# Asking by name for one function table set at the head of six stages

## The reference

```python
log_1m = jnp.where(causal, jax.nn.log_sigmoid(-z), 0.0)          # stick-breaking, gates: log(1 + exp(-|z|))
y = xf * lax.rsqrt(jnp.mean(xf * xf, axis=-1, keepdims=True) + EPS)   # in the kernel exp(-0.5 * log(...))
dt = jax.nn.softplus(dt_raw.astype(jnp.float32) + dt_bias.astype(jnp.float32))
```

## Time and profile before

| | us |
|---|---|
| median of 3 runs | 3015.35 |
| lowest, highest | 3010.44, 3020.8 |
| profiled execution, its own time | 3026.64 |
| its span | 3024.8 |
| TensorE matmuls busy | 2710.7 |
| ScalarE busy | 684.2 |
| VectorE busy | 1305.2 |
| GpSimd busy | 1503.0 |

### The profile page before, as it was taken

One profiled execution on the slowest core, in us unless ns is written; L12 is line 12 of the kernel. 1 busy time (PEld: TensorE's weight loads), 2 busy tenths in 40 slices (PEclk: granted clock), 3 DMA queues, 4 the chain that ended last, 5 costly groups with the idle time before them and its releaser, 6 DMA issues. The chain is left out here.

```text
span 3024.8 us, 33325 instructions
## 1 busy us (share of the span) xinstructions
PE 2710.7 (90%) x11856; PEld 2109.7 (70%) x11856; DVE 1305.2 (43%) x1909; ACT 684.2 (23%) x1008; POOL 1503.0 (50%) x1022
## 2 busy tenths in 40 slices
PE   6897779999988998789988998989997989899996
PEld 4784447888857775468965874858875668678774
DVE  4953333222229999727202415242165213454442
ACT  2003652001133333411022104131022230200002
POOL 2543005666638887256622753416651256466651
PEclk7997789999999998899999998979999999999998
DMA  7531002323212222122320221112320022223221
GB/s 253 181 112 63 1 0 70 98 97 98 98 56 70 83 84 72 43 83 70 98 70 14 98 82 44 58 41 70 98 84 28 22 90 75 64 97 94 87 78 37
DMA packets 230474, 231.17 MB, mean 76 GB/s; under 512 B 9995, under 2 KB 228844, under 8 KB 230252
## 3 DMA queue, kind: packets, MB, share of 16 engines
q1 hardware_dynamic: 225968, 228.74, 23.6%
q10 hardware_dynamic: 4412, 1.24, 0.2%
HBM read 227.86 MB, written 2.10 MB: 76 GB/s over the span
## 5 line engine op out<-in xcount | busy, mean ns | idle before, releaser
L829 POOL TENSOR_SCALAR Wh<-raw 128x2048 fp32r<-128x2048 f32 (+3 forms) x197 | 367.5, 1866 | 1370.7 <-PE PS L873 1129.5
L835 POOL TENSOR_TENSOR Wl<-raw,Wh 128x512 fp32r<-128x512 f32 (+3 forms) x772 | 1026.7, 1361 | 29.2 <-issue 1.6
L873 PE MATMUL PS<-Hh,Wh 128*128 128x512 f32 (+2 forms) x2104 | 842.7, 401 | 117.7 <-DVE Hl L596 54.7
L873 PE MATMUL PS<-Hl,Wh 128*128 128x512 f32 (+2 forms) x2104 | 836.4, 398 | 0.0
L873 PE MATMUL PS<-Hh,Wl 128*128 128x512 f32 (+2 forms) x2104 | 835.3, 397 | 0.0
L873 PEld LDWEIGHTS PS<-Hh,Wh 128*128 128x128 f32 (+2 forms) x2104 | 402.5, 191 | 227.6 <-issue 90.1
L873 PEld LDWEIGHTS PS<-Hh,Wl 128*128 128x128 f32 (+2 forms) x2104 | 401.9, 191 | 90.6 <-issue 1.5
L873 PEld LDWEIGHTS PS<-Hl,Wh 128*128 128x128 f32 (+2 forms) x2104 | 403.1, 192 | 86.7
L873 PE MATMUL PS<-Bh,Wh 128*128 128x512 f32 x688 | 270.2, 393 | 17.8 <-DVE Bl L1851 9.1
L873 PE MATMUL PS<-Bl,Wh 128*128 128x512 f32 x688 | 269.0, 391 | 0.0
L873 PE MATMUL PS<-Bh,Wl 128*128 128x512 f32 x688 | 268.9, 391 | 0.0
(11 more groups left out here) (308 smaller groups left out, 2888.4 us busy)
## 6 DMA issues: line engine op xcount, KB each, us to landing
raw<-in_w_in SPq DMA_DIRECT2D x44, 1024.0 KB, 5.6
raw<-in_w_ff SPq DMA_DIRECT2D x32, 1024.0 KB, 5.3
raw<-in_conv_w_in SPq DMA_DIRECT2D x24, 1024.0 KB, 5.2
raw<-in_ret_w_in SPq DMA_DIRECT2D x24, 1024.0 KB, 5.2
spare<-in_ada_w SPq DMA_DIRECT2D x20, 1024.0 KB, 6.9
raw<-in_w_up SPq DMA_DIRECT2D x20, 1024.0 KB, 5.2
raw<-in_w_out SPq DMA_DIRECT2D x8, 1024.0 KB, 5.1
raw<-in_conv_w_out SPq DMA_DIRECT2D x8, 1024.0 KB, 5.3
```

The source lines that it names most:

```text
L829: pool.tensor_scalar(st.Wh[0:rows, slot, k, 0:g.width], st.raw_slot(slot)[0:rows, k, 0:g.width], 1.0, 1.0, ALU.mult, ALU.mult)
L835: ins = pool.tensor_tensor(st.Wl[0:rows, slot, k, 0:g.width], st.raw_slot(slot)[0:rows, k, 0:g.width], st.Wh[0:rows, slot, k, 0:g.width].b ...
L873: mm = pe.matmul(out, lhs, rhs, start=(k == 0 and n == 0), stop=(k == parts[-1][0] and n == 2))
```

## The change

At the head of ScalarE's program of six stages stands a request for one table set by name. Nothing else is touched.

```diff
+EXP_AND_LOG = "natural_log_exp_and_others"
...
+        act.preload_act_table_set(EXP_AND_LOG)     # attention_part
         for h in range(SH):
             softplus(h)
...
     def _(act):
+        act.preload_act_table_set(EXP_AND_LOG)     # retention_part
         for h in range(RET_HEADS):
             act.wait_ge(pv_done, h + 1)
...
+        act.preload_act_table_set(EXP_AND_LOG)     # gates_parts
         act.wait_ge(biased, 1)
         act.activation(t1, g_f, ACT.Abs)
...
+        act.preload_act_table_set(EXP_AND_LOG)     # mlstm_part
         for h in range(M_HEADS):
             for b in range(NB):
                 act.wait_ge(spread, h + 1)
...
+        act.preload_act_table_set(EXP_AND_LOG)     # steps_parts
         act.wait_ge(free, 1)
         act.activation(st.heads[hs, 4:5], st.heads[hs, 3:4], ACT.Exp).then_inc(rate_in, 1)
...
             act.activation(SQ(c), src[c], ACT.Square).then_inc(squared, 1)
+        act.preload_act_table_set(EXP_AND_LOG)     # group_norm_part
         for g in range(S_GROUPS):
             act.wait_ge(ss_in, g + 1)
```

## The result

The changed kernel takes 2983.64 us (median of 4 runs, 2981.0 to 2984.72) beside 3014.99 for the kernel before (4 runs too): a ratio of 0.9894, interval 0.9875 to 0.9912. A second measurement on another occasion gave 2990.69 beside 3017.22, 0.9906 (0.9882 to 0.9930). So it is faster by 27 to 31 us. The forecast was 22.9 us, a ratio of 0.9924: inside the second interval, just outside the first. The changed kernel's profiled execution took 2981.0 us.

A forecast was written before the change was run, and what follows sets the result against it. ScalarE was taken as far from the bound (TensorE's matmuls 2710.7 of 3024.8 us), so loads count only where TensorE or VectorE waits; stage terms sum to 22.9 us, 3015.35 to 2992.5 us, range 2980 to 3005.

The forecast's parts named there:

- kept set: All stages: the requested set stays past its stage, so four later norms lose their pairs, 8 loads.
- 56 loads: Whole program: table loads fall from 101 to 56, 45 fewer, 57.7 us less of ScalarE's time.
- order of the waits: Attention heads: without the loads, the other attention's maxima on VectorE become the next bound after ScalarE's logarithm.
- Attention 10.6: Attention: 1.28 us in head 0, 0 in head 1, 2.4 in heads 2, 4, 6, 5.7 in 3, 5, 7, 1.28 last norm.
- Norms 5.2: Four norms behind attention and group norm: the load before Exp is worth 1.30 us each, the one before Ln 0.
- Retention 1.3: Retention: only in the last head does VectorE, and then TensorE's next product, wait for ScalarE; 1.3 us.
- mLSTM 3.2: mLSTM heads: 0.8 us at the head, 0.6 in the middle, 1.8 at the end.
- Group norm 1.3: Group norm of y: the request replaces the first load, the second load goes, worth 1.30 us.
- Gates 0: mLSTM gates: VectorE is 1.28 us earlier, but its next convolution waits for TensorE anyway; worth 0.
- Mamba steps 1.3: Mamba steps: VectorE waits for the logarithm and TensorE then for VectorE; one load's 1.28 us.
- upward rival: TensorE's clock: shorter gaps keep it at its higher level, 5 us on top of the forecast, 2987; chance 0.13.
- doubled sum (2980): Whole kernel: counting the Trainium skill's drain with each load, single-load terms double, an estimated 35 us gain, 2980.

The follow-up runs named there:

- norms_too: Changed kernel with the set also requested at the head of the five norms that still load twice and of the Mamba heads: 2983.09 us, 0.9898.
- both: Changed kernel with VectorE's two attention steps swapped and the set also requested in the other norms and the Mamba heads: 2964.35 us beside 3012.20, 0.9854.
- load_at_log: Changed kernel with the set requested again ahead of each logarithm of the attention (8) and of the Mamba steps (1): 2992.38 us, 0.9924.
- only_steps: Kernel before with the request in the Mamba steps alone, one load fewer in the program: 3019.21 us, 1.0012.
- only_attention: Changed kernel with only the attention's request kept of the six: 3000.42 us, 0.9942.
- only_mlstm: Changed kernel with only the mLSTM heads' request kept of the six, 4 loads fewer in the program: 3020.64 us, 1.0005.
- shifted: Kernel before with three loads of the exponential's set between logarithm and exponential of the first norm: 3015.59 us, 1.000.
- load_at_norms: Changed kernel with 12 repeated requests ahead of logarithm and exponential in the attention's four head norms and the mLSTM's two: 2999.55 us, 0.9956.

## Why the prediction came out as it did

The kept set, the 56 loads and the order of the waits came out as forecast. The median lies inside the stated range, near its lower end; the gain is 4 to 8 us more than the sum of 22.9, of which waits explain 1.6 (below). Term by term, measured as waits in the traces, not as stage times:

- *Attention 10.6*: logits to suffix sums (from the end of L1079 to the start of L1087, eight heads) fell from 69.5 to 60.2 us, 9.3. Behind the last norm VectorE's product starts 1.28 sooner, but the output projection 1.00 (TensorE's gap 4.24 instead of 5.24; 1.28 sooner too in norms_too and both, 3.96). Together 10.3. That it comes so close is in part luck, since errors cancelled. Head 0 gave 0.2 instead of 1.28: VectorE's four products behind the maximum start 1.3 us earlier, into GpSimd's subtractions, and take 2.01 us (timeline of changed) where they took 0.90 (before):

```profile
259.76 4.99 POOL L838 TENSOR_TENSOR Wl<-raw,Wh 128x512 fp32r<-128x512 f32 x4
...
263.30 2.01 DVE L1206 TENSOR_TENSOR spare<-spare,squares 128x128 f32<-128x128 f32 x4
```

```profile
265.50 0.90 DVE L1202 TENSOR_TENSOR spare<-spare,squares 128x128 f32<-128x128 f32 x4
```

  Heads 3, 5 and 7 gave 2.4, 2.1 and 2.1 instead of 1.9, since TensorE's transposes ahead of the maxima had waited for the head norm too (0.39 us in head 3). The heads 2, 4, 6 gave 0.8 each, head 1 nothing.
- *Norms 5.2*: 1.28 in each of four gaps, 5.1. *Retention 1.3*: TensorE's gap behind it is 4.33 instead of 5.60. *mLSTM 3.2*: 0.85 + 0.65 + 1.85. *Group norm 1.3*: the gap is 7.79 instead of 9.07, 1.28. *Gates 0*: the convolution beside them took 102.0 us before and after.
- *Mamba steps 1.3* is the mis-sized term. TensorE's gap went from 3.86 to 0.63, 3.2 us, and the stage from 34.0 to 29.2. The forecast took the row of VectorE's wait and moved everything behind it by 1.28, without asking which of these operations had been slowed by GpSimd and whether they still would be. load_at_log and only_steps show it from both sides; in only_attention, only_mlstm and shifted the gap is even 5.30, while the stage is 34.3. Nor is the gain certain: in load_at_norms, which has no load added in this stage, GpSimd's instruction fell a little earlier against VectorE's, the casts ran straight into it (timeline of load_at_norms), TensorE's gap was 4.37 and the stage took 33.4 us:

```profile
2219.08 1.92 POOL L832 TENSOR_SCALAR Wh<-raw 128x2048 fp32r<-128x2048 f32 x1 [4.25 <-PE PS L876]
2219.11 6.06 DVE L1678 CAST Bl<-spare 16x512 fp32r<-16x512 f32 x4
```

The waits sum to 24.5 us, 1.6 over the forecast, and the Mamba steps alone are 1.9 over. The rest of the measured 27 to 31 us, 2 to 7 us, I put down by difference to TensorE's clock, the upward rival, given 0.13 and 5 us; no run isolates it. Time at 1.2 GHz fell from 401 to 354 and 344 us. Part of it repeats: norms 7 and 8 are 3.0 us shorter with the six requests than in each execution with one or none, and the Mamba steps are 1.6 us shorter than in before beyond what their gap explains, with 3 us at 1.2 GHz instead of 7. Part comes and goes without the request, as in the attention, and the mLSTM heads differed by 6.9 us between two executions of the changed kernel. And part goes the other way: the feed-forward of block 3 had its lowest times, 377.1 and 377.2, in two executions without all requests and 382.3 in the changed kernel, though shifted (381.0) and only_steps (384.1) show that it needs no request for that.

Why norms 7 and 8 are faster, where their own loads and gaps are the same, stays open. Of the six requests only the attention's and the retention's stand ahead of them, and the attention's alone left them at 55.9; the retention's, which shortens TensorE's gap there by 1.27, was not tried alone.

The doubled sum (2980) by the drain that the Trainium skill counts with each switch (ScalarE: Activation LUTs, What ACT_TABLE_LOAD costs) was nearer to the first median, but for another reason: no gap got shorter by more than one load's 1.28 where one load went, apart from the collision. The prediction took the profiled execution's 11.3 us over the median for a spread that the runs have; it lies 5.8 us above the highest of them. Since the 22.9 us are a difference, that did not touch them.

## What to carry to other kernels

Where exponentials and logarithms take turns, name the set that holds both, once, where ScalarE waits anyway, and count on the stages behind it as well. Price each load by the idle time of the engine that waits, up to the next bound, and not by 1.28 times their number: of 45 removed loads (57.7 us) waits of 24.5 us came through. Then look at what is late next: here it was the order of two steps on VectorE, and swapping them took 6.3 us more of waiting away.

## What the runs showed of the hardware

- Moving VectorE's work by a few us changes what it costs when GpSimd is busy: four casts took 1.02, 2.74, 4.04 or 6.06 us, four products 0.90 or 2.01. It went once for and once against the change. The Trainium skill (SBUF — State Buffer, Who interferes with whom) describes a port pair shared by the two engines, held for a whole instruction; the products, with two inputs, fit its rule, and the durations agree with a wait of that kind. For an instruction with one input the same section of the Trainium skill lets them contend only in a mode that uses both port pairs. The traces don't name the mode of the casts, but those slowed in before and in load_at_norms end 0.1 to 0.3 us behind the end of one of GpSimd's instructions (2.0 us for one that takes 0.28 otherwise).
- Two executions of the changed kernel agree to 0.1 us in every stage of the table but the mLSTM heads (73.1 and 80.0). Between kernels whose code in a stage is the same, the attention took 173.2 to 180.0 us and the long feed-forward 377.1 to 384.1, by the granted clock.
- In that feed-forward TensorE waits three times for VectorE, 2.56, 2.56 and 3.7 us, in all these kernels. In every execution the falls to 1.2 GHz within it begin in such a wait or at most 1.6 us behind its end, which agrees with the prediction's reading that the grant falls behind gaps. But not every wait is followed by one: only the second in before, all three in the changed kernel. Timeline of TensorE in before, behind that second wait:

```profile
2840.75 0.50 PE L873 MATMUL PS<-Bh,Wh 128*128 128x512 f32 x1 [2.56 <-DVE Bl L2075]
```

- A request for the set that is already there is still a full load of 1283 ns: load_at_log has nine more ACT instructions than the changed kernel, 972 for 963.
